# Delta rule: the triangular inverse's narrow levels on 64x64 stationary sides instead of 32x32

## The chip, the cores and the metric

One core of one Trainium2 chip. The metric is the device time of one execution of the whole program in microseconds; 3 runs of the kernel before were timed.

## The reference

The program computes a small model of two token streams (256 latent and 256 context tokens, 1024 wide): a gated delta-rule mixer, a mixture of 16384 tiny experts, attention, and further mixers. The change touches the delta rule alone. Cut to that:

```python
def gated_delta_chunked(q, k, v, g, beta, s0):     # chunks of 64, heads of 128
    def step(S, inp):
        qc, kc, vc, gc, bc = inp
        gc = jnp.cumsum(gc, axis=-1)
        decay = jnp.exp(jnp.where(incl, gc[..., :, None] - gc[..., None, :], -jnp.inf))
        kk = jnp.einsum('bhid,bhjd->bhij', kc, kc)
        a = eye + jnp.where(strict, kk * decay * bc[..., :, None], 0.0)
        rhs = jnp.concatenate([vc * bc[..., None], kc * (bc * jnp.exp(gc))[..., None]], axis=-1)
        sol = lax.linalg.triangular_solve(a, rhs, left_side=True, lower=True, unit_diagonal=True)
        ...
        return S, o
```

It is run forward and backward over each stream, for 16 heads. The triangular matrix a, unit diagonal plus a strict part, has to be solved for each head, chunk and direction.

## The kernel before, in words

The program is a list of stages, each with a method per engine (pe, dve, act, pool, sp); an engine's instructions stand in the order in which these methods issue them, and semaphores (Count objects P, V, S, G for TensorE, VectorE, ScalarE and GpSimd) carry the dependencies. TensorE is PE, VectorE is DVE, ScalarE is ACT and GpSimd is POOL below.

The stage DeltaNet works in two halves of 8 heads. In each half the projections, convolutions and rows come first, then the chain (pe_chain, act_chain, pool_chain, dve_chain), then gate and output projection. The kernel takes chunks of 128 tokens: a chain runs over 4 steps, i = 0 to 3 (two chunks of each stream), so there are 8 steps in all. In a step four "chains" (two groups of 4 heads, two directions; `self.chains`) are worked on side by side, and every engine goes through them in the same order. A chain has 4 heads, whose 128x128 matrices lie beside each other.

The inverse P of the triangular matrix is built up by blocks: of 2, 4, 8, 16, 32, then 64 and 128. `LEVELS` has the first five. Up to 32 everything lies in compact tiles of 128 partitions x 4 heads x 32 columns: the four diagonal blocks of 32 of a head stand below each other, one in each quarter of the partitions. `self.small[ch]` has four such tiles: Tc (P transposed), Pc (P), Dc (decay times keys times beta) and Xc (a copy of X). `self.blocks[ch]` has, for levels 1 to 4, Dc times the mask of that level.

The head of a step is dve_chain L1335 to L1350: for each chain Dc = D x kk (L1342), times beta (L1344), then Tc = Dc x mask of level 0 (L1346), Tc = identity - Tc (L1348), and Pc = the transpose of Tc in 32x32 blocks (L1350, by the helper dve_turn, L1318). When Dc is there, POOL makes the masked blocks in two products (L1257: level 1, and levels 2 to 4 together), and after those of all four chains the products L1263 (Db) and L1265 (DTm) of each.

A level l (1 to 4) is two phases on PE, over all four chains each: X = block(l) transposed times P (L1051), then, when ACT has copied X to SBUF (L1205), Y = T transposed times X (L1061), and DVE takes Y off P (L1355) and turns P into T (L1357, also recorded as L1318). Each product is 32x32 by 32x32, one per head and quarter, at a tile position (r.start, r.start), so 16 products per chain and phase. Every float32 product is two pairs of a weight load and a matmul in the records. X of a level waits for L1355 of the level before, Y for the turn. After each level DVE has two larger products for one chain (L1361, which waits for Db, and L1364, which waits for DTm). After level 4 come the products with the state (L1069, only for i > 0) and the corners of 64 and 128 in pe_corners (L1123 and on, L1147, L1158, L1169).

The masks come from a table of constants that the host makes (`constants()`); "lev" is loaded on POOL's queue (L683) and cast to bf16 (L884); the table's first `nconst` columns are loaded at the very start (L446).

Of the kernel before, what the change touches and what calls it, by code (L numbers as in the profile page):

```python
# [9 lines left out]
BF16 = mybir.dt.bfloat16  # L10
# [10 lines left out]
def constants():  # L21

    i = np.arange(128)
    r, c = i[:, None], i[None, :]
    parts = {
        "ident": r == c, "le": r <= c, "gt": r > c, "ge": r >= c, "lt": r < c,
        "ones": np.ones((128, 128)), "iota": np.broadcast_to(c, (128, 128)),
        "sel32": (i[:, None] % 32 == np.arange(32)[None, :]) & (np.arange(32)[None, :] < 2),
        "id32": i[:, None] % 32 == np.arange(32)[None, :],
        "par": np.stack([(i // 16) % 2 == 0, (i // 16) % 2 == 1, i < 64, i >= 64], 1),  # L30
        "sel": np.stack([np.broadcast_to(i == h, (128, 128)).T for h in range(8)], 1).reshape(128, 1024),
    }
    t = np.arange(256)
    parts["causal"] = np.concatenate([np.where(t[None, :] <= 128 * n + r, 0.0, NEG) for n in range(2)], 1)
    inv = 10000.0 ** (-np.arange(0, 64, 2, dtype=np.float32) / np.float32(64))
    ang = np.concatenate([(t // 64)[:, None] * inv, (t % 64)[:, None] * inv], 1).astype(np.float32)
    for name, f in (("cos", np.cos), ("sin", np.sin)):
        parts[name] = f(ang).reshape(2, 128, 64).transpose(1, 0, 2).reshape(128, 128)
    r, c = i[:, None] % 32, np.arange(32)[None, :]
    low = [(r // (2 * s) == c // (2 * s)) & ((r // s) % 2 == 1) & ((c // s) % 2 == 0) for s in LEVELS]  # L40
    high = [(r // (2 * s) == c // (2 * s)) & ((r // s) % 2 == 0) & ((c // s) % 2 == 1) for s in LEVELS]
    parts["lev"] = np.concatenate(low + high, 1)
    off, at = {}, 0
    for k, v in parts.items():
        off[k] = (at, v.shape[1])
        at += v.shape[1]
    return np.concatenate([np.asarray(v, np.float32) for v in parts.values()], 1), off
# [569 lines left out]
class DeltaNet(Stage):  # L617
    def __init__(self, k):
# [6 lines left out]
        nl = len(LEVELS)  # L625
        self.lev = k.al(2 * nl * 16).bitcast(BF16).rearrange("p (d l m) -> p d l m", d=2, l=nl)
        self.cw = k.al2(32, 5)
# [7 lines left out]
        self.norm = Norm(self, range(4), self.hT, A, B, scr)  # L635
        self.tmp = k.al(2 * nl * 32)
        self.cr = k.al(5 * 128)
# [3 lines left out]
        k.top = work  # L641
        self.bufs = {(hg, d): [k.al3(1, 4, 128)[:, 0] for _ in range(8)] for hg in range(2) for d in range(2)}
        self.pads = [k.al(520).rearrange("p (s t) -> p s t", s=2) for _ in range(2)]
        self.cvs = [k.al(512) for _ in range(2)]
        self.sqs = k.al(128)
        self.chains = list(self.bufs)
        self.bv = {ch: k.al3(1, 4, 128)[:, 0] for ch in self.chains}
        self.small = {ch: [b[n].rearrange("p h m -> p (h m)")[:, a:a + 128].rearrange("p (h m) -> p h m", h=4)
                           for n, a in ((3, 0), (3, 128), (3, 256), (5, 0))] for ch, b in self.bufs.items()}
        self.blocks = {ch: b[0].rearrange("p h m -> p (h m)").rearrange("p (l h m) -> p l h m", l=4, h=4)  # L650
                       for ch, b in self.bufs.items()}
        k.top = work
# [26 lines left out]
    def pool(self, e):  # L679
        k, i, G = self.k, self.k.i, self.G  # L680
        self.enter(e)
        o = k.off["lev"][0]
        e.dma_start(self.tmp, i["consts"][:, o:o + 2 * len(LEVELS) * 32]).then_inc(*self.l_lev.up("l"))  # L683
        e.dma_start(self.cr[0:32, :].rearrange("c (t p) -> c t p", t=5),
# [294 lines left out]
    def corners(self, l, d):  # L979
# [6 lines left out]
        return out  # L986

    def quarters(self):
        return [slice(32 * b, 32 * b + 32) for b in range(4)]
# [24 lines left out]
    def pe_chain(self, e, half):  # L1014
        P, V, S, G = self.P, self.V, self.S, self.G
        for i in range(4):
# [26 lines left out]
            for l in range(1, 5):  # L1043
                for ch in self.chains:
                    Tc, Pc, Dc, Xc = self.small[ch]
                    X = self.two(ch)[0][:, 256:384].rearrange("p (h n) -> p h n", h=4)
                    e.wait_ge(*G.at(key(f"lev{l}", ch)))
                    e.wait_ge(*V.at(key(f"P{l - 1}", ch)))
                    for h in range(4):
                        for r in self.quarters():  # L1050
                            m = e.matmul(X[r, h, :], self.blocks[ch][r, l - 1, h, :], Pc[r, h, :], start=True, stop=True,  # L1051
                                         tile_position=(r.start, r.start))
                    m.then_inc(*P.up(key(f"X{l}", ch)))
                for ch in self.chains:
                    Tc, Pc, Dc, Xc = self.small[ch]
                    Y = self.two(ch)[0][:, 384:512].rearrange("p (h n) -> p h n", h=4)
                    e.wait_ge(*S.at(key(f"X{l}", ch)))
                    e.wait_ge(*V.at(key(f"T{l - 1}", ch)))
                    for h in range(4):
                        for r in self.quarters():  # L1060
                            m = e.matmul(Y[r, h, :], Tc[r, h, :], Xc[r, h, :], start=True, stop=True, tile_position=(r.start, r.start))  # L1061
                    m.then_inc(*P.up(key(f"Y{l}", ch)))
# [170 lines left out]
    def pool_chain(self, e, half):  # L1233
# [3 lines left out]
        for i in range(4):  # L1237
# [15 lines left out]
            for ch in self.chains:  # L1253
                Dc, lev = self.small[ch][2], self.lev[:, ch[1]]
                e.wait_ge(*V.at(key("Dc", ch)))
                for a, b in ((1, 2), (2, 5)):
                    e.tensor_tensor(self.blocks[ch][:, a - 1:b - 1], Dc.unsqueeze(1).to_broadcast([128, b - a, 4, 32]),  # L1257
                                    lev[:, a:b].unsqueeze(2).to_broadcast([128, b - a, 4, 32]), MUL).then_inc(*G.up(key(f"lev{a}", ch)))
                for l in (3, 4):
                    G.mark(key(f"lev{l}", ch))  # L1260
            for ch in self.chains:
# [47 lines left out]
    def dve_decay(self, e, half, i, ch):  # L1309
# [3 lines left out]
                        MUL).then_inc(*self.V.up((half, i, ch, "gL")))  # L1313

    def dve_turn(self, e, src, dst):

# [3 lines left out]
    def dve_chain(self, e, half):  # L1320
# [5 lines left out]
        for i in range(4):  # L1326
# [8 lines left out]
            for ch in self.chains:  # L1335
# [9 lines left out]
                e.wait_ge(*V.now())  # L1345
                e.tensor_tensor(Tc, Dc, self.lev[:, ch[1], 0].unsqueeze(1).to_broadcast([128, 4, 32]), MUL).then_inc(*V.up())  # L1346
                e.wait_ge(*V.now())
                e.tensor_tensor(Tc, self.k.const("id32").unsqueeze(1).to_broadcast([128, 4, 32]), Tc, SUB).then_inc(*V.up(key("T0", ch)))  # L1348
                e.wait_ge(*V.now())
                self.dve_turn(e, Tc, Pc).then_inc(*V.up(key("P0", ch)))  # L1350
            for l in range(1, 5):
                for ch in self.chains:
# [3 lines left out]
                    e.wait_ge(*V.now())  # L1356
                    self.dve_turn(e, Pc, Tc).then_inc(*V.up(key(f"T{l}", ch)))  # L1357
                ch = self.chains[l - 1]
                D, DT, kk = self.bufs[ch][1], self.bufs[ch][2], self.keys(ch)
# [1650 lines left out]
```

## Time and profile before

| | |
|---|---|
| runs | 4565.18, 4558.86 and 4569.99 us (median 4565.18) |
| profiled execution | 4564.14 us |
| its span | 4562.3 us |
| mean granted TensorE clock | 0.905 |
| PE, weight loads, DVE, ACT, POOL busy | 3697.2, 2016.6, 2554.4, 971.4, 1243.6 us |
| the four chains of the first half | about 340 to 640 us of the span |
| the four chains of the second half | about 894 to 1191 us |

A row names the line of the kernel, the engine, the operation and its shapes. For PE the first pair (32*32) is the stationary side, partitions by columns. "PEld" are weight loads, which overlap PE. "Idle before" is the time in which the engine had nothing to do, with what ended it; "issue" is a wait for nothing that the profile shows. PEclk is the clock that TensorE was granted, 1.00 being 2.4 GHz and 0.50 1.2 GHz. The ends of matmuls are modelled, and the start of a next one is the surer number.

### The profile page before, as it was taken

How to read it: one execution, taken by the hardware profiler on the slowest of the kernel's cores; microseconds unless marked ns; L12 is line 12 of the kernel's file. 1: busy time of each engine (PE TensorE's matmuls, PEld its weight loads, DVE VectorE, ACT ScalarE, POOL GpSimd, SP SyncE). 2: the span in 40 equal slices, each digit the busy share in tenths (PEclk: the TensorE clock that was granted, in tenths of full speed). 3: DMA queues.
4: the chain of work that ended last, by engine and by line, in shares of the span. 5: the costliest groups of instructions: out<-in, count | busy, mean ns of one | idle time of the engine just before them, and what ended most of it. 6: DMA issues, size and time to landing. Idle time of an engine off the chain costs nothing.

```text
span 4562.3 us, 59212 instructions
## 1 busy us (share of the span) xinstructions
PE 3697.2 (81%) x22791; PEld 2016.6 (44%) x22791; DVE 2554.4 (56%) x5869; ACT 971.4 (21%) x2601; POOL 1243.6 (27%) x1271
## 2 busy tenths in 40 slices
PE   6796779967879997777777779887777789865999
PEld 2446654466544442222222235543222358432684
DVE  1244552545446677777677645767776338357341
ACT  0132311332122222222222212322222121010100
POOL 1004320143003444444444410344444010037000
PEclk7697889968889999999999989999999889976999
DMA  9420002100149999999999952999999334320443
GB/s 370 138 63 5 3 30 74 56 3 3 45 164 379 408 415 420 418 418 409 412 413 405 420 227 65 358 416 418 417 413 417 110 96 139 120 74 0 135 151 123
DMA packets 269478, 1043.49 MB, mean 229 GB/s; under 512 B 19394, under 2 KB 103596, under 8 KB 170896
## 3 DMA queue, kind: packets, MB, share of 16 engines
q0 software_dynamic: 114736, 815.52, 43.9%
q1 hardware_dynamic: 154464, 224.18, 14.6%
q8 instruction: 184, 3.01, 0.3%
q14 instruction: 94, 0.77, 0.0%
HBM read 1038.55 MB, written 1.08 MB: 228 GB/s over the span
## 4 chain that ended last, share of the span: by engine, by line
PE 50%; DMA 26%; DVE 11%; issue 5%; ACT 4%; POOL 3%; DVEq 0%; POOLq 0%; ACTq 0%; SPq 0%
DMA arena<-in_peer_uv,arena 24%; PE psum L261 13%; PE psum L1664 11%; PE psum L299 4%; PE psum L723 4%; PE psum L1622 3%; PE psum L762 2%; DVE arena L1799 2%; PE psum L212 2%; DMA arena<-in_ada_w 2%; PE psum L1061 1%; PE psum L1051 1%; POOL arena L2849 1%; PE psum L1083 1%; PE psum L1069 1%
## 5 line engine op out<-in xcount | busy, mean ns | idle before, releaser
L1664 PE MATMUL psum<-arena 128*128 128x512 f32 x3072 | 1462.6, 621 | 392.7 <-ACT arena L1699 389.0
L1799 DVE SCALAR_TENSOR_TENSOR arena<-arena 128x1024 bf16<-128x1024 f32 x768 | 940.6, 1225 | 524.6 <-DMA arena<-in_peer_uv,arena 493.4
L1757 POOL DMA_INDIRECT arena<-in_peer_uv,arena x768 | 853.7, 1112 | 1186.7 <-PE psum L1664 1045.7
L1664 PEld LDWEIGHTS psum<-arena 128*128 128x128 f32 x3072 | 575.8, 196 | 1230.4 <-ACT arena L1699 634.9
L261 PE MATMUL psum<-ring,arena 128*128 128x512 f32 (+2 forms) x1408 | 598.1, 589 | 30.1 <-DVE arena L2678 9.1
L261 PEld LDWEIGHTS psum<-ring,arena 128*128 128x128 f32 x1408 | 271.0, 201 | 351.3 <-issue 324.9
L1692 ACT ACTIVATE arena<-arena 128x2 f32<-128x2 f32 x384 | 78.2, 204 | 1250.0 <-DVE arena L1799 1250.0
L299 PE MATMUL psum<-arena,ring 128*128 128x256 f32 x1408 | 313.6, 384 | 9.0 <-DVE arena L2673 7.7
L1699 ACT ACTIVATE arena<-consts,arena 128x128 f32<-128x128 f32 x768 | 268.4, 394 | 223.8 <-DVE arena L1811 223.0
L299 PEld LDWEIGHTS psum<-arena,ring 128*128 128x128 f32 x1408 | 269.8, 193 | 50.9 <-issue 8.0
L723 PE MATMUL psum<-arena,ring 128*128 128x512 f32 x512 | 231.4, 607 | 1.6 <-issue 1.6
L212 PE MATMUL psum<-consts,arena 128*128 128x128 f32 (+3 forms) x705 | 117.9, 314 | 141.4 <-DVE arena L362 75.4
L1622 PE MATMUL psum<-arena,ring 128*128 128x128 f32 (+3 forms) x704 | 181.9, 409 | 9.1 <-ACT arena L1438 7.4
L212 PEld LDWEIGHTS psum<-consts,arena 128*128 128x128 f32 (+3 forms) x705 | 94.5, 162 | 198.9 <-issue 103.9
L1622 PEld LDWEIGHTS psum<-arena,ring 128*128 128x128 f32 x704 | 119.9, 199 | 77.5 <-issue 49.5
L723 PEld LDWEIGHTS psum<-arena,ring 128*128 128x128 f32 x512 | 97.5, 195 | 114.5 <-issue 114.5
L2842 POOL TENSOR_TENSOR arena<-arena 128x256 f32<-128x256 f32 x32 | 32.5, 1017 | 339.3 <-DVE arena L2866 339.3
L1051 PE MATMUL psum<-arena 32*32 32x32 f32 x4096 | 68.6, 228 | 69.6 <-issue 45.2
L329 ACT ACTIVATE arena<-x_res 128x1024 f32<-128x1024 f32 x10 | 10.6, 1058 | 507.0 <-DVE x_res L2685 319.3
L1247 POOL MEMSET arena<- 128x512 f32 x8 | 4.2, 522 | 402.0 <-ACT arena L876 402.0
L762 PE MATMUL psum<-ring,arena 128*128 128x512 f32 x256 | 110.4, 593 | 1.6 <-ACT arena L859 1.6
L1061 PE MATMUL psum<-arena 32*32 32x32 f32 x4096 | 69.3, 234 | 50.1 <-issue 50.1
(400 smaller groups left out, 4029.0 us busy)
## 6 DMA issues: line engine op xcount, KB each, us to landing
arena<-in_ada_w SPq DMA_DIRECT2D x48, 1024.0 KB, 14.4
ring<-in_ffn_w_up SPq DMA_DIRECT2D x44, 1024.0 KB, 5.1
ring<-in_dn_w_in SPq DMA_DIRECT2D x24, 1024.0 KB, 5.3
ring<-in_peer_w_query SPq DMA_DIRECT2D x22, 1024.0 KB, 7.4
ring<-in_ffn_w_down SPq DMA_DIRECT2D x20, 1024.0 KB, 5.0
arena<-in_peer_uv,arena POOLq DMA_INDIRECT x768, 12.9
ring<-in_ev_w_in SPq DMA_DIRECT2D x10, 1024.0 KB, 5.1
ring<-in_dn_w_out SPq DMA_DIRECT2D x8, 1024.0 KB, 4.9
```

Source lines behind the costliest of these rows:

```text
L212: return e.transpose(out, in_, self.k.const("ident")[0:n, 0:n])
L261: m = e.matmul(o, self.hT[:, k0 + k, t * 128:(t + 1) * 128], w[:, k, :], start=k0 + k == 0, stop=k0 + k == self.KC - 1)
L299: m = e.matmul(self.bank(c)[:, 0:self.nt], w[:, k, j * 128:(j + 1) * 128], self.hT[:, k, 0:self.nt], start=k == 0, stop=k == self.KC - 1)
L723: m = e.matmul(k.banks[j % 4], w[:, q, j % 2 * 128:(j % 2 + 1) * 128], self.hT[:, q, :], start=q == 0, stop=q == 7)
L762: m = e.matmul(k.banks[t * 2 + nh], self.oT[:, k0 + q, t * 128:(t + 1) * 128], w[:, q, nh * 512:(nh + 1) * 512], start=k0 + q == 0, stop=k ...
L1051: m = e.matmul(X[r, h, :], self.blocks[ch][r, l - 1, h, :], Pc[r, h, :], start=True, stop=True, tile_position=(r.start, r.start))
L1061: m = e.matmul(Y[r, h, :], Tc[r, h, :], Xc[r, h, :], start=True, stop=True, tile_position=(r.start, r.start))
L1622: m = e.matmul(k.banks[j % 2][:, 0:w_], w[:, n, c % 2 * 128:(c % 2 + 1) * 128], self.hT[:, n, a * 128:b * 128], start=n == 0, stop=n == 7)
L1664: m = e.matmul(k.banks[4 + t % 2 * 2 + nh], self.diag[g % self.ND], self.vsl[g % self.NS][:, nh * 512:(nh + 1) * 512], start=u % 8 == 0 an ...
L1699: e.activation(self.diag[g % self.ND], k.const("ident"), ACT.Copy, bias=0.0, scale=self.cf[u % 2][:, s:s + 1]).then_inc(*S.up(("dg", g)))
L1757: e.indirect_dma_start(self.uv[g % self.NS], None, self.table(), bass.IndirectOffsetOnAxis(ap=self.eid[u % 6][:, s:s + 1], axis=0)).then_i ...
L1799: e.scalar_tensor_tensor(self.junk[g % 2], self.us[g % self.NS], 1.0, self.h[:, u // 8, :], MUL, MUL, accum_out=self.a[u % 2][:, s:s + 1]) ...
```

## The change

The 32x32 stationary sides of X and Y in levels 1 to 4 become 64x64, so that one product serves two quarters of the partitions. The 64 columns hold, beside the block of a quarter, zeros where the other quarter's columns are. X and Y, and the moving sides, keep their shapes. So there are 8 products per chain and phase instead of 16, at two tile positions instead of four.

To have the stationary sides in that form, the masks "lev" are 64 wide; POOL makes each level's block by one product of 256 elements a partition (Dc is read twice, side by side), four per chain, each with a mark of its own; and DVE makes a wide copy of T (`wideT`) with the new method dve_wide, in the head and after each of the levels 1 to 3. Level 0 and the copy use new constants, "low0", "high0" and "odd". The tiles move: the blocks of levels 3 and 4 lie over the buffers of the convolution (`idle`), which rest while the chains run.

```diff
@@ constants()
+        "low0": (i[:, None] % 2 == 1) & (i[:, None] % 32 == np.arange(32)[None, :] + 1),
+        "high0": (i[:, None] % 2 == 0) & (i[:, None] % 32 == np.arange(32)[None, :] - 1),
+        "odd": (i[:, None] // 32) % 2 == np.arange(2)[None, :],
...
-    r, c = i[:, None] % 32, np.arange(32)[None, :]
+    r, c = i[:, None] % 64, np.arange(64)[None, :]
@@ DeltaNet.__init__
-        self.lev = k.al(2 * nl * 16).bitcast(BF16).rearrange("p (d l m) -> p d l m", d=2, l=nl)
+        self.lev = k.al(2 * nl * 32).bitcast(BF16).rearrange("p (d l m) -> p d l m", d=2, l=nl)
...
-        self.tmp = k.al(2 * nl * 32)
+        self.tmp = k.al(2 * nl * 64)
...
+        self.idle = k.arena[:, k.top:k.top + 2048]
...
+        self.small = {ch: [cols(b[5], 128, 32), cols(b[3], 256, 32), cols(b[3], 384, 32), cols(b[5], 0, 32)] for ch, b in self.bufs.items()}
+        self.wideT = {ch: cols(b[3], 0, 64) for ch, b in self.bufs.items()}
+        self.blocks = {}
+        for n, ch in enumerate(self.chains):
+            for l in range(1, 5):
+                a = flat(self.bufs[ch][0]) if l < 3 else self.idle[:, 512 * n:512 * n + 512]
+                self.blocks[ch, l] = a[:, (l - 1) % 2 * 256:(l - 1) % 2 * 256 + 256].rearrange("p (h m) -> p h m", h=4)
@@ DeltaNet.pool
-        e.dma_start(self.tmp, i["consts"][:, o:o + 2 * len(LEVELS) * 32]).then_inc(*self.l_lev.up("l"))
+        e.dma_start(self.tmp, i["consts"][:, o:o + 2 * len(LEVELS) * 64]).then_inc(*self.l_lev.up("l"))
@@ pe_chain
                     for h in range(4):
-                        for r in self.quarters():
-                            m = e.matmul(X[r, h, :], self.blocks[ch][r, l - 1, h, :], Pc[r, h, :], start=True, stop=True,
+                        for r in self.halves():
+                            m = e.matmul(X[r, h, :], self.blocks[ch, l][r, h, :], Pc[r, h, :], start=True, stop=True,
                                          tile_position=(r.start, r.start))
...
                     for h in range(4):
-                        for r in self.quarters():
-                            m = e.matmul(Y[r, h, :], Tc[r, h, :], Xc[r, h, :], start=True, stop=True, tile_position=(r.start, r.start))
+                        for r in self.halves():
+                            m = e.matmul(Y[r, h, :], self.wideT[ch][r, h, :], Xc[r, h, :], start=True, stop=True,
+                                         tile_position=(r.start, r.start))
@@ pool_chain
-                for a, b in ((1, 2), (2, 5)):
-                    e.tensor_tensor(self.blocks[ch][:, a - 1:b - 1], Dc.unsqueeze(1).to_broadcast([128, b - a, 4, 32]),
-                                    lev[:, a:b].unsqueeze(2).to_broadcast([128, b - a, 4, 32]), MUL).then_inc(*G.up(key(f"lev{a}", ch)))
-                for l in (3, 4):
-                    G.mark(key(f"lev{l}", ch))
+                for l in range(1, 5):
+                    e.tensor_tensor(self.blocks[ch, l].rearrange("p h (j m) -> p h j m", j=2), Dc.unsqueeze(2).to_broadcast([128, 4, 2, 32]),
+                                    lev[:, l].rearrange("p (j m) -> p j m", j=2).unsqueeze(1).to_broadcast([128, 4, 2, 32]),
+                                    MUL).then_inc(*G.up(key(f"lev{l}", ch)))
@@ new in DeltaNet
+    def dve_wide(self, e, ch):
+
+        return e.tensor_tensor(self.wideT[ch].rearrange("p h (j m) -> p h j m", j=2), self.small[ch][0].unsqueeze(2).to_broadcast([128, 4, 2, 32]),
+                               self.k.const("odd").unsqueeze(1).unsqueeze(3).to_broadcast([128, 4, 2, 32]), MUL)
@@ dve_chain
-                e.tensor_tensor(Tc, Dc, self.lev[:, ch[1], 0].unsqueeze(1).to_broadcast([128, 4, 32]), MUL).then_inc(*V.up())
+                e.tensor_tensor(Tc, Dc, self.k.const(("low0", "high0")[ch[1]]).unsqueeze(1).to_broadcast([128, 4, 32]), MUL).then_inc(*V.up())
                 e.wait_ge(*V.now())
-                e.tensor_tensor(Tc, self.k.const("id32").unsqueeze(1).to_broadcast([128, 4, 32]), Tc, SUB).then_inc(*V.up(key("T0", ch)))
+                e.tensor_tensor(Tc, self.k.const("id32").unsqueeze(1).to_broadcast([128, 4, 32]), Tc, SUB).then_inc(*V.up())
                 e.wait_ge(*V.now())
                 self.dve_turn(e, Tc, Pc).then_inc(*V.up(key("P0", ch)))
+                self.dve_wide(e, ch).then_inc(*V.up(key("T0", ch)))
...
                     self.dve_turn(e, Pc, Tc).then_inc(*V.up(key(f"T{l}", ch)))
+                    if l < 4:
+                        e.wait_ge(*V.now())
+                        self.dve_wide(e, ch).then_inc(*V.up(key(f"T{l}", ch)))
```

## Rows read from the trace of the kernel before

**Rows 1.** The page, costliest groups: the two rewritten lines
```profile
L1051 PE MATMUL psum<-arena 32*32 32x32 f32 x4096 | 68.6, 228 | 69.6 <-issue 45.2
...
L1061 PE MATMUL psum<-arena 32*32 32x32 f32 x4096 | 69.3, 234 | 50.1 <-issue 50.1
```

**Rows 2.** Timeline of one level: start us, duration us, engine, line, shapes, count, idle before
```profile
985.73 1.00 PE L1051 MATMUL psum<-arena 32*32 32x32 f32 x57 [1.54 <-issue]
...
989.19 1.01 PE L1061 MATMUL psum<-arena 32*32 32x32 f32 x58 [1.54 <-issue]
```

**Rows 3.** The page: instructions of PE, and its instruction queue (packets, MB)
```profile
PE 3697.2 (81%) x22791; PEld 2016.6 (44%) x22791; DVE 2554.4 (56%) x5869; ACT 971.4 (21%) x2601; POOL 1243.6 (27%) x1271
...
q8 instruction: 184, 3.01, 0.3%
```

**Rows 4.** Timeline of the head of step i = 1, first half, DVE and POOL
```profile
420.37 0.29 DVE L1342 TENSOR_TENSOR arena<-arena 128x128 f32<-128x128 f32 x1 [7.91 <-ACT arena L1200]
...
421.06 1.45 POOL L1257 TENSOR_TENSOR arena<-arena 128x128 f32<-128x128 f32 x2 [16.10 <-DVE arena L1344]
...
422.01 0.66 DVE L1342 TENSOR_TENSOR arena<-arena 128x128 f32<-128x128 f32 x1
...
424.03 0.65 DVE L1342 TENSOR_TENSOR arena<-arena 128x128 f32<-128x128 f32 x1
```

**Rows 5.** Chain of waits: last X of level 1, end of Y of level 4, first and last step
```profile
360.59 0.65 PE psum L1051 x32
...
385.34 0.36 PE psum L1123 x24
...
1131.46 0.42 PE psum L1051 x26
...
1157.85 2.43 PE psum L1069 x5
```

**Rows 6.** L1169: timeline, its durations (min/median/max), and the stretch's busy times and clock
```profile
948.92 1.12 PE L1169 MATMUL psum<-arena 64*64 64x64 f32 x16 [0.23 <-ACT arena L1222]
...
L1169 PE MATMUL psum<-arena x256: 218/311/367, 396.3 to 1174.4; 64*64 64x64 f32 x128
...
948.90:950.10 1.20, 1.18 (x17) 1.08 (x17) 0.00 (x0) 0.72 (x3) 1.20 (x2) 0.50 0.06 14
```

**Rows 7.** The gate projection: timeline, and busy times (PE, PEld, DVE, ACT, POOL) and clock
```profile
190.85 13.88 PE L261 MATMUL psum<-ring,arena 128*128 128x64 f32 x64 [0.84 <-ACT arena L339]
...
193.00:196.00 3.00, 3.00 (x16) 3.00 (x16) 0.00 (x0) 0.00 (x0) 0.00 (x0) 0.50 0.00 0
```

**Rows 8.** Busy times and clock of ten microseconds of narrow levels
```profile
510.00:520.00 10.00, 5.09 (x338) 4.74 (x342) 3.47 (x12) 1.11 (x4) 2.32 (x3) 0.50 0.02 4
```

**Rows 9.** Chain of waits behind level 4 of the first step
```profile
385.70 2.14 issue
```

**Rows 10.** Lines of DVE and POOL: count, durations ns min/median/max, first and last start, forms
```profile
L1346 DVE TENSOR_TENSOR arena<-arena x32: 291/291/1103, 352.6 to 1130.2; 128x128 f32<-128x128 f32 x32
...
L1361 DVE TENSOR_TENSOR arena<-arena x32: 516/517/1569, 363.8 to 1158.5; 128x384 f32<-128x384 f32 x32
...
L1355 DVE TENSOR_TENSOR arena<-arena,psum x128: 247/250/289, 361.7 to 1157.9; 128x128 f32<-128x128 f32 x128
...
L1318 DVE STREAM_TRANSPOSE arena<-arena x160: 311/311/315, 354.1 to 1158.2; 128x128 f32<-128x128 f32 x160
...
L1364 DVE TENSOR_TENSOR arena<-arena,psum x32: 673/676/679, 365.2 to 1158.9; 128x512 f32<-128x512 f32 x32
...
L1263 POOL TENSOR_TENSOR arena<-arena x32: 816/822/1144, 360.8 to 1138.0; 128x384 f32<-128x384 f32 x32
...
L1265 POOL TENSOR_TENSOR arena<-arena,consts x32: 1254/1262/1589, 361.6 to 1138.8; 128x512 f32<-128x512 f32 x32
...
L1257 POOL TENSOR_TENSOR arena<-arena x64: 472/745/966, 353.5 to 1130.8; 128x128 f32<-128x128 f32 x32, 128x384 f32<-128x384 f32 x32
```

**Rows 11.** Chain of waits: the state's products behind level 4, step i = 1
```profile
452.19 5.89 PE psum L1069 x16
```

More of the change, by code:

```diff
@@ L647, in __init__ @@
         self.bv = {ch: k.al3(1, 4, 128)[:, 0] for ch in self.chains}
[L648 to L651, printed above, removed]
+        flat = lambda a: a.rearrange("p h m -> p (h m)")
+        cols = lambda a, at, n: flat(a)[:, at:at + 4 * n].rearrange("p (h m) -> p h m", h=4)
+        self.small = {ch: [cols(b[5], 128, 32), cols(b[3], 256, 32), cols(b[3], 384, 32), cols(b[5], 0, 32)] for ch, b in self.bufs.items()}
[5 more added lines that the diff above has]
+                self.blocks[ch, l] = a[:, (l - 1) % 2 * 256:(l - 1) % 2 * 256 + 256].rearrange("p (h m) -> p h m", h=4)
         k.top = work
@@ L986, in corners, with halves @@
         return out
+    def halves(self):
+        return [slice(64 * b, 64 * b + 64) for b in range(2)]
     def quarters(self):
```

## The prediction

> **What bounds the kernel now.** I read the page first, then the chain of waits over the delta-rule stretch, the waits of TensorE, the order of time of single levels, and the granted clock. The two lines that the change rewrites, L1051 (X) and L1061 (Y), are only 69 us busy each, but have 45 and 50 us of idle time before them with the releaser "issue" [rows 1]. All of it lies in 8 steps (2 halves, 4 steps of i); one step has 4 levels, and a level is a phase of X for the four chains and a phase of Y for the four chains, 16 products of two instruction pairs each, so 128 pairs (weight load and matmul) a phase.
>
> From one stall to the next it is 3.46 us, and in 1.54 of them TensorE stands without waiting for any engine [rows 2]; the 128 pairs of a phase take the other 1.92, 15 ns each. The instruction queue moves blocks of 16.4 KB (3.01 MB in 184 packets), and 3.01 MB over TensorE's 2 x 22791 instructions are 66 bytes each, so a block holds about 250 instructions: the 128 pairs of a phase [rows 3]. I read the stall as the next block arriving: the narrow levels are bound by the delivery of instructions, at one block in about 3.5 us. Neither DVE nor ACT is late there.
>
> Before the levels comes a head that another engine bounds. L1342, L1344, L1346, L1348 and the turn L1318 run on DVE chain after chain, 2.02 us from one L1342 to the next, and X of level 1 starts for the last chain when the last turn is done [rows 4]. Counted from that start to the end of Y of level 4, the eight steps take 24.75, 23.93, 27.02, 28.72, 26.58, 26.08, 25.05 and 26.39 us, 26.07 on average [rows 5] (the first and the last of the eight stand there).
>
> **The change, part by part.**
>
> *X and Y on TensorE.* 128 pairs a phase become 64, with a 64x64 stationary side and 32 moving columns on two tiles. Instructions: half a block a phase, so one block in two phases; the stall goes. What is late next is the array. The nearest rows are L1169's: 64x64 stationary, 64 moving, alternating between the same two tiles, 16 pairs in 1.12 us of which the last is 0.311: 54 ns a pair, at a granted clock of 0.50, the 1.2 GHz level [rows 6]. There load and matmul are equally wide, so the row alone doesn't say which sets the 54. The gate projection does: stationary 128 columns, moving 64, at 0.50: 13.88 us for 64 pairs, 217 ns each [rows 7], twice what 64 columns take on one tile by the row before (107 ns), so there the weight load of 128 columns sets the pace, and not the moving side. A 64-column load is then 107 ns at this clock, on two tiles side by side 54 ns a pair, whatever the moving side. A phase becomes 64 x 54 = 3.46 us: as long as now. The bounds: below, if only the 32 moving columns counted, 27 ns, half of rows 6; above, 107 ns, if the two tiles' loads didn't run together. I take 54, because rows 6 have exactly these tiles and this width.
>
> *The clock.* It is 0.50 in the levels now [rows 8]. The gate projection kept TensorE busy for 14 us without a gap, bound by weight loads, and stayed at 0.50 all the while [rows 7]. The new phases are of that kind, so I keep 0.50.
>
> From the last X of level 1 to the end of Y of level 4: 16 x 54 ns + 7 phases x 3.46 = 25.1 us against 26.07, a gain of 1.0 us a step, 8 us in all. In the first step the next line, L1123, waits another 2.1 us on "issue" [rows 9]; they go too.
>
> *The wide copy on DVE (dve_wide).* 256 elements a partition, both inputs in SBUF. Between L1346's 291 ns for 128 elements and L1361's 517 for 384, it costs 0.40 us where nothing disturbs it. It stands in DVE's queue between one chain's turn and the next chain's work: four times in the head, and four in each of levels 1 to 3. In the levels DVE then needs 4 x 1.0 (L1355 0.25, turn 0.31, copy 0.40, and the waits of 0.03) + 0.52 + 0.68 = 5.2 us a level [rows 10], under TensorE's 6.9, so it is hidden there. Behind it stand L1355 of the next chain, for which X of the next level waits: that comes at 1.1 + 3.3 = 4.4 us from the start of a Y phase, and X of the last chain is due at 3.46 + 3 x 0.86 = 6.0. If the phases were half as long, that cover would be gone and DVE would set 5.2 a level.
>
> *The blocks on POOL and the head.* Two products a chain (128 and 384 elements, 0.47 and 0.96 us) become four of 256. By 0.82 us for 384 and 0.47 for 128 [rows 10] one is 0.64, a chain 2.6 instead of 1.43 us. Now the trace shows that such a product of POOL and a DVE product with both inputs in SBUF don't run together: L1342 is 0.29 us while POOL rests and 0.65 while POOL works, and ends 0.16 us after POOL does [rows 4]. POOL rested in 0.6 of each 2.0 us of the head (1.45 us busy); now it would never rest. Walking one chain through, with DVE and POOL taking turns: Dc at 0, POOL's first product ends at 0.7 and lets L1348 through, the second ends at 1.5 and lets the copy through, the third (late by the copy) at 2.4 lets the next L1342 through, the fourth at 3.2 lets the next L1344 through, and the next Dc is there at 3.3. So a chain takes 3.3 instead of 2.0 us. X of level 1 of the last chain waits for three such chains: +4.0 us a step, 32 us over 8 steps, all on the path. Bounds: +0.4 a chain, 1.2 a step, if the lock cost nothing more than now; +1.7 a chain (each of five DVE products behind a full 0.64), 5 a step. I take 4.0, since rows 4 show every meeting of the two ending as a wait.
>
> *The rest.* POOL ends its blocks 4 to 6 us later, and L1263 and L1265 (0.82 and 1.26 us, four chains) move with them into levels 1 and 2. L1361 and L1364 wait for them behind each level, and the wide copies meet them: a wait of up to 1.26 us a copy in level 1. With 1.6 us to spare in each level I cost it at nothing; without that cover it is 1 to 3 us a step. DMAs: the masks' load on POOL's queue is 320 KB instead of 160 (128 partitions x 640 columns x 4 bytes) and lies under the norm; the constants' load grows by 66 columns, 34 KB, ahead of the loads of x and ctx on the same queue: no more than 0.1 us. The cast of the masks to bf16 has 320 more columns, 0.3 us by L1361's 517 ns for 384. Together +0.4.
>
> **Sum**, on the profiled execution's 4564.1 us (span 4562.3; the median of the runs is 1.0 above it): +32 - 8 - 2.1 + 0.4 = +22: 4586 us.
>
> Against the trace stands a page. The Trainium skill, "TensorE: Matmul & The Clock Gate", section "LDWEIGHTS (loading the stationary operand)", agrees that the columns and not the rows price a load, but puts it at columns / 1.2 ns: an estimate of 53 ns for 64 columns, 27 ns a pair on two tiles. The trace's float32 loads take twice that at the low clock, and the measurement decides.
>
> **The rivals.**
>
> *The weight load is cheaper than I read it (faster).* For it: no row has 64x64 with 32 moving. Against it: the gate projection. At 27 ns a pair TensorE needs 3.5 us a level and DVE's 5.2 decide. From the last X of level 1: 1.1 us to the first L1355, 3 x 5.2 + 1.5 for meetings with POOL, 1.3 for the rest of the last Y phase: 19.5, that is 6.6 less than 26.07 and, with the head's 4.0, 2.6 a step less: -21 - 2.1 + 0.4: 4541 us. It decides below 46 ns a pair, where the 464 pairs of a step have given back the head's 4.0 us and 1.1 more (8 x 1.1 = 9 us, 0.2%). Chance 0.12. By the page's figure above, this is the case that comes true.
>
> *The clock rises in the levels (faster).* Pairs of 27 ns as well, and L1069 behind them, 5.89 us at the low clock [rows 11], would be up to 2.9 shorter in six steps: 4524. But then TensorE would work 3.5 of 5.2 us, hardly more steadily than now at 0.50. 0.05.
>
> *The head gets only the plain 0.4 us a chain (no change).* +10 - 8 - 2.1 + 0.4: 4564. For it: POOL's products may leave room that I don't see. Against it: L1342, and L1346 at 1.10 us beside a long POOL product [rows 10]. 0.17.
>
> *The meetings in levels 1 and 2 come on the path (slower still).* 1 to 3 us a step: 4594 to 4610. 0.13. The Trainium skill, "SBUF — State Buffer", section "Who interferes with whom", has a DVE instruction with two SBUF inputs block fully against POOL's reads; by it this is the case if POOL's queue is still long when the first copies of level 1 come, and rows 4 agree with the block itself.
>
> *The two loads don't run together.* 107 ns a pair, +24 us a step: about 4780. 0.03; rows 6 speak against it.
>
> **How the numbers follow.** A difference under 0.2% (9 us) can't be told from none here. My own case, 4575 to 4602, has 0.50. Slower: 0.50 + 0.13 + 0.03 = 0.66; within 0.2%: 0.17; faster: 0.17. The range leaves out the rising clock and half of the cheap load below, and the loads one after another and the far end of the meetings above: 4543 to 4607.
>
> **What would show it.** In the profile after: L1051 and L1061 with half the instructions, no "issue" before them, phases of about 3.5 us and pairs 54 ns apart; the clock still 0.50; L1257 with 128 products of 0.6 us or more, L1342 and the copy longer than 0.4 in the head, and 3.3 us from chain to chain. Wrong, if pairs are 27 ns apart, if "L1355 <- L1061" vanishes from DVE's waits, or if the head grows by less than 2 us.

## The result, and the profile after

The changed kernel takes 4579.5 us (median of 7 runs, 4577.31 to 4583.02) against 4565.18 us before: a ratio of 1.0035, with a 95% interval of 1.0023 to 1.0047. It is slower by 14 us, 0.35%. Forecast were 4586 us, a range of 4543 to 4607 and "slower" as the likeliest. The profiled execution took 4580.9 us (span 4579.1), 16.8 us more than the profiled one before.

The page of the changed kernel has the line of X (now L1063) at half the instructions; L1270 are POOL's products for the blocks. The columns are those of rows 1.

```profile
L1063 PE MATMUL psum<-arena 64*64 64x32 f32 x2048 | 113.5, 281 | 46.7 <-DVE arena L1335 46.7
...
L1270 POOL TENSOR_TENSOR arena<-arena 128x256 f32<-128x256 f32 x128 | 93.5, 758 | 129.2 <-DVE arena L1361 129.2
```

Its part on DMA queues has TensorE's instructions (packets, MB, share):

```profile
q8 instruction: 152, 2.49, 0.2%
```

"issue" is gone from the idle time before X, and 32 of 184 blocks of instructions with it. In its place stands the turn of the head (L1335). The chain of waits shows the head and the levels of the second step (i = 1, first half); L1073 is Y.

```profile
424.03 0.69 DVE arena L1359
...
424.74 0.66 DVE arena L1361
...
425.75 0.65 DVE arena L1365
...
426.65 0.54 DVE arena L1329
427.19 0.69 DVE arena L1359
...
433.20 1.06 PE psum L1063 x16
434.26 3.41 PE psum L1073 x64
437.68 3.41 PE psum L1063 x64
441.09 3.41 PE psum L1073 x64
...
454.74 3.41 PE psum L1073 x64
458.15 6.28 PE psum L1082 x16
```

Each phase takes 3.41 us: 53.3 ns a pair, without a gap. From the last X of level 1 (433.20) to the end of level 4 (458.15) it is 24.95 us, and it is 24.95 to 24.98 in all eight steps, where before it went from 23.93 to 28.72 [rows 5]. In the head the chains are 3.16 us apart (424.03 to 427.19) instead of 2.02 [rows 4]. The timeline of the head shows why; POOL's row holds four products:

```profile
421.59 0.29 DVE L1359 TENSOR_TENSOR arena<-arena 128x128 f32<-128x128 f32 x1 [7.91 <-ACT arena L1213]
...
422.28 2.95 POOL L1270 TENSOR_TENSOR arena<-arena 128x256 f32<-128x256 f32 x4 [15.89 <-DVE arena L1361]
422.56 0.65 DVE L1365 TENSOR_TENSOR arena<-consts,arena 128x128 f32<-128x128 f32 x1
...
423.48 0.54 DVE L1329 TENSOR_TENSOR arena<-arena,consts 128x256 f32<-128x256 f32 x1
423.95 0.76 DVE L1359 TENSOR_TENSOR arena<-arena 128x128 f32<-128x128 f32 x1
424.74 0.65 DVE L1361 TENSOR_TENSOR arena<-arena 128x128 f32<-128x128 f32 x1
```

and all of POOL's products by their line, with the least, the median and the longest in ns:

```profile
L1270 POOL TENSOR_TENSOR arena<-arena x128: 664/721/854, 353.3 to 1149.5; 128x256 f32<-128x256 f32 x128
```

The same L1359 is 0.29 us before POOL starts and 0.76 beside it; L1361, L1365 and the copy (L1329) are long as well. POOL is busy for 2.95 of each 3.16 us. The head, from its first product (421.59) to the last X of level 1, is 11.61 us instead of 7.89, and in the first step 13.30 instead of 9.58: +3.72 us both times.

The clock in the levels is what it was [rows 8], although TensorE now has no idle time at all:

```profile
440.00:450.00 10.00, 10.00 (x193) 10.00 (x191) 9.04 (x21) 1.66 (x6) 3.84 (x4) 0.50 0.01 2
```

So the 16.8 us of the trace are: heads 8 x 3.72 = +29.8; levels 8 x (24.96 - 26.07) = -8.9; behind level 4 in the two steps with i = 0, -2.1 and -1.8 (the first from 385.34 to 391.94 before and from 389.16 to 393.65 now, where L1147 starts, now L1160). The sum is +17.0. In the second of these steps the end of level 4 is taken, in the kernel before, where the chain of waits leaves TensorE (936.97); TensorE is through with Y only when L1123 starts at 937.65. So 0.7 us of the -1.8 is the level's own, and behind level 4 it is -3.2 in all. That sum and trace agree to 0.2 us is partly luck: from the last level 4 to the end of the span, where the kernels don't differ, the twelve traces of this document take between 3401.4 and 3408.2 us (3404.6 before, 3405.5 in the changed kernel).

### The profile page after: what moved, and what is told of

It reads as the page before. It is cut to its first block, busy times and chain, and to the rows that moved or that the text cites. A ratio compares the mean times of both kernels' runs of the same rounds, so it can differ in the third digit from the quotient of the medians.

```text
span 4579.1 us, 51212 instructions
## 1 busy us (share of the span) xinstructions
PE 3790.0 (83%) x18695; PEld 2114.3 (46%) x18695; DVE 2652.1 (58%) x5997; ACT 972.4 (21%) x2601; POOL 1305.5 (29%) x1335
## 4 chain that ended last, share of the span: by engine, by line
PE 52%; DMA 25%; DVE 12%; ACT 4%; POOL 3%; issue 3%; another core or an unknown queue 0%; DVEq 0%; POOLq 0%; ACTq 0%
DMA arena<-in_peer_uv,arena 23%; PE psum L264 13%; PE psum L1685 12%; PE psum L302 4%; PE psum L732 4%; PE psum L1643 3%; PE psum L771 2%; PE psum L1073 2%; DVE arena L1820 2%; PE psum L215 2%; PE psum L1063 2%; DMA arena<-in_ada_w 2%; POOL arena L2870 1%; PE psum L1096 1%; POOL arena L1778 1%
## 5 line engine op out<-in xcount | busy, mean ns | idle before, releaser
L1778 POOL DMA_INDIRECT arena<-in_peer_uv,arena x768 | 863.3, 1124 | 1176.2 <-PE psum L1685 1037.7
L1063 PE MATMUL psum<-arena 64*64 64x32 f32 x2048 | 113.5, 281 | 46.7 <-DVE arena L1335 46.7
L1063 PEld LDWEIGHTS psum<-arena 64*64 64x64 f32 x2048 | 108.8, 209 | 49.7 <-POOL arena L1270 48.7
L1270 POOL TENSOR_TENSOR arena<-arena 128x256 f32<-128x256 f32 x128 | 93.5, 758 | 129.2 <-DVE arena L1361 129.2
L2863 POOL TENSOR_TENSOR arena<-arena 128x256 f32<-128x256 f32 x32 | 32.5, 1017 | 340.5 <-DVE arena L2887 340.5
```

The costliest lines, as they stand in the source:

```text
L1063: m = e.matmul(X[r, h, :], self.blocks[ch, l][r, h, :], Pc[r, h, :], start=True, stop=True, tile_position=(r.start, r.start))
L1270: e.tensor_tensor(self.blocks[ch, l].rearrange("p h (j m) -> p h j m", j=2), Dc.unsqueeze(2).to_broadcast([128, 4, 2, 32]), lev[:, l].rear ...
L1778: e.indirect_dma_start(self.uv[g % self.NS], None, self.table(), bass.IndirectOffsetOnAxis(ap=self.eid[u % 6][:, s:s + 1], axis=0)).then_i ...
```

## The experiments

The theory: TensorE's part of the change trades one bound, the delivery of instructions, for another that is nearly as dear, the loading of 64-column weights, and gains a little; the head pays for it, because DVE's and POOL's products there take turns. The rivals: the wide products themselves cost the time; the moving side sets their pace; the head is long by the copy's own length or by POOL alone; the stall before was each phase's own and had nothing to do with the number of instructions. All times below are medians; ratios are to the kernel before, timed beside each, with 95% intervals.

**Narrow products on the wide tiles.**

```diff
-                        for r in self.halves():
-                            m = e.matmul(X[r, h, :], self.blocks[ch, l][r, h, :], Pc[r, h, :], ...
+                        for b, r in enumerate(self.quarters()):
+                            at = slice(b % 2 * 32, b % 2 * 32 + 32)
+                            m = e.matmul(X[r, h, :], self.blocks[ch, l][r, h, at], Pc[r, h, :], ...
```
(and Y in the same way, from wideT)

> The changed kernel with the 32x32 products of before, which read their 32 columns out of the wide tiles; POOL's four products, the wide copy and everything else of the change stay. Theory (the change costs in the head, 3.2 instead of 2.0 us a chain, and gains a little in the levels): the head stays as in the changed kernel, the levels fall back to 26.1 us a step with 1.5 us stalls on issue, so some 9 to 13 us slower than the changed kernel: 4588 to 4593 us. Rival (the 64-wide products are what costs, and the head is paid for elsewhere): back to the time of before, 4565 us.

Measured: 4594.0 us, ratio 1.006 (1.0043 to 1.0077). The stalls are back. What ended the idle time before L1064, the X product, and before L1075, the Y product, in us and times:

```profile
  issue: 85.5, 55
...
  issue: 106.3, 54
```

These sums count each stall once for the weight loads and once for the matmuls; the matmuls alone stood 39.4 and 51.3 us, 90.7 over the eight steps, as against 95.3 in the kernel before [rows 1]. So the head's price alone is about 28 us, and the 64-wide products by themselves give back 14.

**16 moving columns.**

```diff
-  m = e.matmul(X[r, h, :], self.blocks[ch, l][r, h, :], Pc[r, h, :], ...
+  m = e.matmul(X[r, h, 0:16], self.blocks[ch, l][r, h, :], Pc[r, h, 0:16], ...
```
(and Y)

> The changed kernel with 16 instead of 32 moving columns in X and Y of levels 1 to 4 (half of each product is left out); the stationary sides stay 64x64. Theory (the loads of 64 columns set the pace, 53 ns a pair): phases stay 3.41 us and the time 4579 us, within 3 us. Rival (the moving side sets the pace): a pair takes 27 ns, DVE then sets 5.2 us a level instead of 6.8, some 5 us a step less: about 4540 us.

Half of each product is left out here. Measured: 4578.4 us, ratio 1.003 (1.0018 to 1.0042), one microsecond from the changed kernel. The chain of waits, same step:

```profile
434.14 3.41 PE psum L1073 x64
```

Half of the moving side changes nothing: the phase is the loads' time. The rival of the moving side falls, and with it the forecast's case of a cheap weight load. The stationary sides compared here are square (32x32, 64x64, 128x128), so these runs don't tell a load's columns from its rows.

**POOL: level 1 first.**

```diff
-            for ch in self.chains:
-                e.wait_ge(*V.at(key("Dc", ch)))
-                for l in range(1, 5):
-                    (block of level l)
-            for ch in self.chains:
-                (Db, DTm)
+            for l in range(1, 5):
+                for ch in self.chains:
+                    if l == 1:
+                        e.wait_ge(*V.at(key("Dc", ch)))
+                    (block of level l)
+                for ch in {2: self.chains[0:1], 3: self.chains[1:2], 4: self.chains[2:4]}.get(l, []):
+                    (Db, DTm)
```

> The changed kernel with POOL's order changed: in the head only the products of level 1 for the four chains, then those of level 2, one chain's Db and DTm, level 3, and so on. Theory (in the head DVE's products with two inputs in SBUF stand behind POOL's products, four of them a chain): with one POOL product a chain the head goes from 3.2 to about 2.5 us a chain, 2 us a step: about 4563 us, and L1359 and L1361 are back near 0.3 us. Rival (the copy's own length and the queue of DVE make the head long): unchanged, 4579 us; it would be slower if level 2 came late.

Measured: 4556.9 us, ratio 0.9983 (0.9974 to 0.9993): 23 us less than the changed kernel, and just faster than the kernel before. The head's timeline (L1360 and L1362 are here what L1359 and L1361 are above, L1271 POOL's product, L1330 the copy):

```profile
419.14 0.78 POOL L1271 TENSOR_TENSOR arena<-arena 128x256 f32<-128x256 f32 x1 [15.99 <-DVE arena L1362]
419.42 0.65 DVE L1366 TENSOR_TENSOR arena<-consts,arena 128x128 f32<-128x128 f32 x1
...
420.34 0.38 DVE L1330 TENSOR_TENSOR arena<-arena,consts 128x256 f32<-128x256 f32 x1
420.64 0.28 DVE L1360 TENSOR_TENSOR arena<-arena 128x128 f32<-128x128 f32 x1
420.95 0.29 DVE L1362 TENSOR_TENSOR arena<-arena 128x128 f32<-128x128 f32 x1
```

With one POOL product a chain only L1366, which meets it, is long (0.65); the others are back at 0.28 and 0.29. The chains are 2.18 us apart (L1360 at 420.64, the next at 422.82). No instruction of DVE was changed here, so it is POOL's products beside them that cost 1 us a chain. The expected 2.5 us a chain, 4563 us in all, was too much. The order changes more than the head, though: against the kernel before, the trace's heads are 6.2 us longer over the eight steps (8.66 for 7.89 in the step above), so the 8.8 us by which the time is below that kernel's come from the levels and what lies behind them.

**The copy on ScalarE** (POOL as in the changed kernel).

```diff
-                self.dve_wide(e, ch).then_inc(*V.up(key("T0", ch)))        # and after levels 1 to 3
+                    e.wait_ge(*V.at(key(f"T{l - 1}", ch)))                 # in act_chain, before each level
+                    for j in range(2):
+                        e.activation(self.wideT[ch]...[:, :, j, :], self.small[ch][0], ACT.Copy, bias=0.0,
+                                     scale=self.k.const("odd")[:, j:j + 1]).then_inc(*S.up(key(f"W{l - 1}", ch)))
```

> The changed kernel with the wide copy of T made on ScalarE instead of VectorE, in two activations a chain with the column of odd as the scale; POOL's four products stay. Theory (the head is long because DVE's and POOL's products with SBUF inputs take turns, and the copy is one of five DVE products there): the head becomes that of the kernel with X alone wide, 2.7 instead of 3.2 us a chain, 1.4 us a step: about 4568 us; the levels stay at 25.0 us a step. Rival (POOL's four products alone set the head): it stays 3.2 us a chain and the time 4579 us.

Measured: 4569.4 us, ratio 1.0019 (1.0009 to 1.0028): 10 us less than the changed kernel, 7 by the two ratios. The chains are 2.72 us apart (DVE's first product, L1364, starts at 421.36 and 424.08), and a head is 1.37 us shorter (10.24 for 11.61), 11 us over the eight. So the copy costs 0.4 us a chain and POOL's three further products in the head the larger part; the head needs both to be as long as it was. The rival of POOL alone falls.

**Both out of the head.** The two edits above together.

> The changed kernel with both costs of the head taken out: the wide copy on ScalarE, and POOL's products of level 1 first. Theory: the head is that of before within 0.2 us a step, so only TensorE's part of the change is left: 25.0 instead of 26.1 us a step from the last X of level 1 to the end of level 4 and 2 us less in each of the two steps with i = 0: 12 to 13 us under the kernel before, 4552 us. Rival (TensorE's part gains nothing, and the order of POOL gave more than the head): 4565 us, or under 4545.

Measured: 4546.7 us, ratio 0.9959 (0.9945 to 0.9972), 5 us under the expectation. The runs lie between 4535.9 and 4554.2, and the profiled one is the second fastest (4538.0), so its trace can show a part of the 5 us and not settle them. One part is here: the first Y phase is shorter than the others, because the head ends while the clock is still at 1.00, and the clock falls during that phase.

```profile
425.62 0.66 PE psum L1063 x16
426.27 2.62 PE psum L1073 x64
428.89 3.41 PE psum L1063 x64
```

The stretches of the same run, with columns as in rows 8 (the granted clock is the third from the end):

```profile
425.00:426.20 1.20, 0.58 (x20) 0.62 (x22) 0.43 (x2) 1.04 (x5) 1.20 (x2) 1.00 0.00 0
426.20:428.00 1.80, 1.80 (x55) 1.80 (x53) 1.08 (x4) 0.94 (x4) 1.80 (x4) 0.75 0.07 14
428.00:430.00 2.00, 2.00 (x43) 2.00 (x42) 1.64 (x6) 1.82 (x7) 2.00 (x3) 0.50 0.00 0
```

This is so in three of the eight steps (the first Y phase is 2.59, 2.79 and 2.84 us from its start to the next X, and 3.41 or 3.42 in the other five): 2.0 us in all. With the last products of level 1, which meet the full clock oftener, the levels are 3.6 us shorter than the changed kernel's. In the changed kernel the clock has fallen in all eight steps before the last X of level 1 starts (in the step i = 1 at about 429.4, 3.8 us before it). In the kernel before it falls in that step at about the same time, 1.1 us after the last X of level 1.

**Half of the narrow products, in the kernel before.**

```diff
-                        for r in self.quarters():
+                        for r in self.quarters()[0:2]:
```
(X and Y)

> The kernel before with only the first two of the four quarters in X and Y of levels 1 to 4: half of the narrow products is left out, the other products stay 32x32. Theory (narrow levels are bound by the delivery of instructions, 256 in 3.46 us): a level has one block instead of two, so it takes about 3.5 us instead of 7, where DVE's own 3.3 us a level are just below: 11 to 13 us a step less: 4462 to 4480 us. Rival (each phase has a stall of its own of 1.5 us, whatever it holds): a level is 2 x 2.5 us, some 7 us a step less: about 4505 us.

Half of each X and Y is left out. Measured: 4463.4 us, ratio 0.9787 (0.977 to 0.9803). The chain of waits in one step:

```profile
415.82 1.71 PE psum L1061 x64
417.53 0.96 PE psum L1051 x36
418.49 0.31 issue
418.80 0.95 PE psum L1051 x28
419.75 1.71 PE psum L1061 x64
```

With half of the instructions, but phases as before, the stalls of 1.5 us are gone save for some 0.3 to 0.6 us: they are not each phase's own. A phase is 1.71 us, 26.7 ns a pair: two tiles, each with a 32-column load of 53 ns, half of the 53.3 ns that a pair of 64 columns takes on two tiles.

**X alone wide.** (Y from Tc in 32x32, no copy.)

```diff
-                        for r in self.halves():
-                            m = e.matmul(Y[r, h, :], self.wideT[ch][r, h, :], Xc[r, h, :], ...
+                        for r in self.quarters():
+                            m = e.matmul(Y[r, h, :], Tc[r, h, :], Xc[r, h, :], ...
```

> The changed kernel with only X on 64x64 sides; Y is done with 32x32 sides out of Tc, and the wide copy is gone. Theory (two separate bounds: a wide phase is bound by weight loads at 3.41 us, narrow ones by the delivery of instructions, 256 in 3.46 us, against 1.75 us of work): a level has 192 pairs, 1.5 blocks, so both bounds give about 5.2 us a level instead of 6.8; from the last X of level 1 to the end of level 4 about 18.5 us instead of 25, the head about 2.9 us a chain: 4520 us, between 4512 and 4532. Rival (the stall belongs to every narrow phase and not to the blocks of instructions): Y phases take 3.46 us again and only the copy is saved: about 4573 us.

Measured: 4546.4 us, ratio 0.9953 (0.9937 to 0.997): a gain, but outside the 4512 to 4532 that I gave. The chain of waits of the step i = 1:

```profile
430.12 1.07 PE psum L1063 x16
431.18 1.52 PE psum L1073 x101
432.71 0.76 issue
433.47 0.63 PE psum L1073 x27
434.10 3.56 PE psum L1063 x64
437.66 1.86 PE psum L1073 x128
...
451.60 4.34 PE psum L1081 x16
```

From 430.12 to 451.60 it is 21.5 us, not 18.5. The 18.5 is about what the array's work alone comes to: 1.07 for the last X, three wide phases of 3.41 and four narrow ones of 1.75. In the chain the three wide phases take 10.9 us instead of 10.2 (each is at least 0.15 us longer than alone, 3.56 for 3.41), and the four narrow ones 2.9, 1.9, 2.9 and 1.9 instead of 7.0 together: two of them still hold a stall of 0.7 us on "issue". I had taken the two bounds level by level. Over the whole stretch it is 16 + 3 x 64 + 4 x 128 = 720 pairs, and by 128 in 3.46 us their delivery alone is 19.5 us (an estimate from rows 2). The head was right (2.7 us a chain, 2.9 expected).

**X alone wide, level 1 first; Y alone wide, copy on ScalarE.** The first is the edit above with POOL's new order. The second keeps X, POOL and the masks of levels 1 to 4 of before, and does Y out of wideT, which ScalarE writes.

> X alone on 64x64 sides, no wide copy, and POOL's order with the products of level 1 first. Theory: one POOL product a chain in the head, so 2.0 us a chain as before; levels of 21.5 us a step as with X alone wide: 4546 less 8 x 3 x 0.7 us, about 4529 us, faster than both kernels. Rival (the later products of POOL come on the path, since a level now takes only 5.4 us): no gain over 4546 us, with waits of X on POOL in levels 2 to 4.

> Only Y on 64x64 sides, with the wide copy on ScalarE; X, the masks and POOL's two products are those of before. Theory: the head is that of before, 2.0 us a chain, and the levels are those of the kernel with X alone wide, 21.5 us a step instead of 26.1, since wide and narrow phases share the two bounds: about 4529 us. Rival (the gain of the kernel with X alone wide came from the missing copy and not from mixing): no better than 4560 us.

Measured: 4523.3 us, ratio 0.9919 (0.9902 to 0.9935), and 4518.4 us, ratio 0.9907 (0.9891 to 0.9924). Both have the head of before (7.66 and 7.88 us for 7.89 in the step i = 1) and mixed levels, and both are under the expected 4529, by 6 and 11 us. The trace of Y alone wide is 46.9 us under the one before: 35.9 in the levels, which the expectation had, 7.0 between the steps, and 4.0 outside the chains, of which 3.1 behind the last step, where the kernels don't differ. With Y wide (L1070) and X narrow (L1060) the stalls are nearly gone, from 421.53 to 442.62 it is 21.1 us:

```profile
422.18 3.56 PE psum L1070 x64
425.74 1.86 PE psum L1060 x128
427.60 3.56 PE psum L1070 x64
431.15 1.86 PE psum L1060 x128
...
438.06 0.23 issue
```

**Two chains wide, two narrow, in every phase.** On top of "both out of the head".

```diff
+                        for r in (self.halves() if ch[0] == 0 else self.quarters()):
+                            m = e.matmul(Y[r, h, :], (self.wideT[ch] if ch[0] == 0 else Tc)[r, h, :], Xc[r, h, :], ...
```
(and X, from the wide block's 32 columns where ch[0] is 1)

> As the kernel with the wide copy on ScalarE and level 1 first, but only the two chains of the first group of heads use 64x64 sides, in X and in Y; the other two do 32x32 products, so each phase has 96 pairs, 32 wide and 64 narrow. Theory (each bound is met within a phase: 2 x 0.85 + 2 x 0.46 = 2.6 us of array time, 2.6 us of instructions): no stall, 7 phases of 2.65 to 2.8 us, about 19.5 us a step instead of 21.1 with Y alone wide: 4506 to 4512 us. Rival (changing between tile widths twice a phase costs as much as the stalls that it saves, or narrow bursts stall again): not below 4518 us.

Measured: 4517.6 us, ratio 0.9891 (0.9877 to 0.9906), no better than Y alone wide within the intervals. Here the rival's first half held:

```profile
434.28 2.85 PE psum L1064 x96
437.13 2.85 PE psum L1074 x96
```

A phase of 32 wide pairs (1.71 us) and 64 narrow ones (0.87 at 13.6 ns) is 2.85 us, 0.27 more than its parts, for two changes of width. Few stalls were left to save: TensorE's matmuls stand 5.6 us on "issue" in the levels of all eight steps here and 6.2 with Y alone wide, so the changes of width take what the better mix might have given. The expected 4506 to 4512 us was missed. The Trainium skill, "TensorEngine Tiling (Array Packing)", section "Key Properties", says that changing the tiling mode drains TensorE; these runs don't show the draining itself, but they agree that a change has a price, about 0.13 us.

## Why the prediction was right

The mechanism was the forecast's, and its size was on the high side: the forecast is a small difference of large terms, +22 us, and +16.8 came in the traces and +14 in the medians.

*What bounds the kernel.* The reading of the stall as the delivery of instructions is borne out by the half products, where the stalls go with the number of instructions, and by the changed kernel, where they are gone with half of it. That it is the delivery and not another thing that comes with every 250 instructions is still an inference from the queue's blocks [rows 3]; nothing here delivers them faster. The Trainium skill, "Runtime: NRT & Kernel Launch", section "Instruction fetch mechanics", has the fetch in 16 KiB blocks and calls its cost mostly hidden; in stretches of 15 ns a pair this trace shows 1.54 us of each 3.46 open.

*The pair's price.* Forecast 54 ns, measured 53.3, and the run with 16 moving columns shows that it is the load's. The clock stayed at 0.50, as the gate projection suggested [rows 7]. Levels: 25.1 us forecast, 24.96 measured; -8 us, and it was -8.9. One of the forecast's eight lengths is too short: the fifth, 26.58, ends where the chain of waits leaves TensorE (936.97) and not where L1123 starts (937.65). It is 27.3, and with it the levels' gain is 9.6.

*The head.* Forecast 3.3 us a chain and +4.0 us a step, measured 3.16 and +3.72: 29.8 us for 32. The walk through one chain was right: the four DVE products that it put behind a POOL product are the four long ones (L1365, the copy, the next L1359 and L1361), and L1363 is 0.29 us. So the upper bound, with all five behind one, wasn't reached. The walk's spacing of POOL's products, 0.8 to 0.9 us, was a little wide: four take 2.95 and a rest of 0.21. POOL's product of 256 elements is 0.66 us at the least and 0.72 in the median, for 0.64.

*The small terms.* Behind level 4 both steps with i = 0 get shorter, by 3.2 us together, or 3.9 on the forecast's count of the fifth step; the forecast had only the first, 2.1, since the stall of the second was 0.6 on the chain and it left that out. The sum of the traces' terms is 5.3 us under the forecast: 2.2 of them are the head, 1.8 this, 0.9 the levels, and 0.4 the loads and masks. Whether these last cost anything can't be told: no term of 0.4 us stands out from traces that differ by microseconds where nothing was changed.

*What was costed at nothing.* The meetings of copy and POOL in levels 1 and 2 are there, up to 1.14 us for one copy, and hidden, as forecast: TensorE has no gap in the phases.

```profile
435.82 1.14 DVE L1329 TENSOR_TENSOR arena<-arena,consts 128x256 f32<-128x256 f32 x1
```

*The rivals.* Cheap loads: gone by the 16 columns. Rising clock: 0.50 in the levels of all eight steps. A head that costs only the copy: measured +1.14 us a chain, but level 1 first shows that this rival names what a better order of POOL would have given (+0.16 a chain). Loads one after another: 53.3 ns.

## What to carry to other kernels

Fewer instructions help only down to the next bound: a block-diagonal stationary side halves the instructions but doubles the columns that each load brings, and with short moving sides the load is the time. Two bounds of that kind are best mixed: with the head kept short, one of the two products wide and the other narrow gave ratios of 0.9919 and 0.9907, both wide 0.9983 and 0.9959. And price what a wider operand asks of the engines that make it where they are on the path: products that POOL needs only later should not stand beside DVE's products in the stretch that DVE bounds.

## What had not been expected

A change between 64- and 32-wide tiles costs about 0.13 us. And a head that is 4 us shorter than the changed kernel's let the first Y phase begin at the full clock in three of eight steps (2.62 for 3.41 us in one of them). In phases that loads set, a later fall of the clock is a gain, and the long head hid it: there the clock had fallen before the last X of level 1 in every step. What had been expected, and is worth keeping beside it: in the levels TensorE was busy for 24 us without a gap and stayed at the 1.2 GHz level (10.00 of 10 us busy at a granted clock of 0.50), in phases that weight loads set.
